# A trunk of two layers on one NeuronCore: the last four weight units of three stages taken tile by tile, with the next stage's norm and transposes between them

## What is computed

```python
def rmsnorm(x, g):
    xf = x * lax.rsqrt(jnp.mean(x * x, axis=-1, keepdims=True) + EPS)
    return xf * g
x = x + conv_ssd_mixer(rmsnorm(x, g0), ...)          # ends in  mixed @ w_out
x = x + swiglu(rmsnorm(x, g1), w_gate, w_up, w_down) # ends in  hidden @ w_down
x = x + diff_attention(rmsnorm(x, g2), ...)          # begins with h @ w_qkv, ends in o @ w_o
h = rmsnorm(x, g3)
logits = h @ w_router                                # 8 experts, the top 2 of each token
x = x + moe_swiglu(h, logits, w_gate_e, w_up_e, w_down_e)
```

## Time and profile before

| | |
|---|---|
| median of 3 runs | 2142.2 us (2140.28 to 2142.95) |
| the profiled execution, its own time | 2140.16 us |
| its span, first to last instruction | 2138.4 us |
| TensorE matmul busy | 2063.0 us, 96% of the span |
| TensorE weight load busy | 1863.9 us |
| VectorE, ScalarE, GpSimd busy | 523.8, 451.5, 487.4 us |
| mean granted TensorE clock | 0.989 of full speed |

### The profile page before, as it was taken

The page is one execution under the profiler, slowest core; times in us unless marked ns, Lnnn a source line. Parts: engine busy times, 40 slices in busy tenths (PEclk is TensorE's granted clock), DMA queues, the critical chain, the costliest instruction groups (busy, mean ns, idle before and its releaser), DMA issues. The chain is left out here.

```text
span 2138.4 us, 32363 instructions
## 1 busy us (share of the span) xinstructions
PE 2063.0 (96%) x13867; PEld 1863.9 (87%) x13867; DVE 523.8 (24%) x987; ACT 451.5 (21%) x896; POOL 487.4 (23%) x246
## 2 busy tenths in 40 slices
PE   7999999999999999988999999999999999999995
PEld 6787778888888878866779999999999999999995
DVE  4534662200000028768340000100101010000102
ACT  4333223332222233358220000000000000000000
POOL 3456564355455434510210000000000000000000
PEclk9999999999999999999999999999999999999998
DMA  7952213233333322310049779888888888898893
GB/s 246 306 163 79 69 59 99 79 100 97 99 94 94 101 83 89 104 35 1 20 168 337 236 251 306 300 304 280 304 282 303 302 300 284 286 310 290 278 343 119
DMA packets 326108, 406.40 MB, mean 190 GB/s; under 512 B 11360, under 2 KB 272554, under 8 KB 325962
## 3 DMA queue, kind: packets, MB, share of 16 engines
q1 hardware_dynamic: 323658, 395.90, 56.1%
q0 software_dynamic: 2304, 8.39, 1.0%
HBM read 373.06 MB, written 31.20 MB: 189 GB/s over the span
## 5 line engine op out<-in xcount | busy, mean ns | idle before, releaser
L875 POOL TENSOR_TENSOR w_lo<-raw,w_hi 128x1024 fp32r<-128x1024 f32 (+1 forms) x159 | 387.9, 2446 | 475.7 <-ACT w_hi L654 475.7
L1456 PE MATMUL ps<-xT,w_gate 128*128 128x132 f32 (+1 forms) x2816 | 356.4, 280 | 4.6 <-issue 3.9
L1456 PE MATMUL ps<-xT,w_up 128*128 128x132 f32 (+1 forms) x2816 | 354.4, 279 | 0.0
L1456 PEld LDWEIGHTS ps<-xT,w_gate 128*128 128x128 f32 x2816 | 340.2, 191 | 5.3 <-issue 4.4
L1463 PE MATMUL ps<-hid,w_down 128*128 128x132 f32 (+1 forms) x2816 | 338.9, 279 | 0.0
L1456 PEld LDWEIGHTS ps<-xT,w_up 128*128 128x128 f32 x2816 | 338.8, 190 | 0.0
L1463 PEld LDWEIGHTS ps<-hid,w_down 128*128 128x128 f32 x2816 | 330.9, 190 | 0.4
L1791 DVE TENSOR_TENSOR hid<-ps,silu_g 128x160 f32<-128x160 f32 x176 | 57.1, 324 | 867.3 <-ACT silu_g L1565 867.3
L1565 ACT ACTIVATE silu_g<-ps 128x160 f32<-128x160 f32 x176 | 53.4, 303 | 934.8 <-PE ps L1456 928.5
L341 PE MATMUL ps<-act_a_hi,w_hi 128*128 128x512 f32 x568 | 226.3, 398 | 0.0
L343 PE MATMUL ps<-act_a_hi,w_lo 128*128 128x512 f32 x568 | 221.2, 390 | 0.0
(11 more groups left out here) (317 smaller groups left out, 2100.6 us busy)
## 6 DMA issues: line engine op xcount, KB each, us to landing
w_gate<-in_moe_w_gate SPq DMA_DIRECT2D x88, 1024.0 KB, 5.5
w_up<-in_moe_w_up SPq DMA_DIRECT2D x88, 1024.0 KB, 8.2
w_down<-in_moe_w_down SPq DMA_DIRECT2D x88, 1024.0 KB, 10.7
raw<-in_even_w_in SPq DMA_DIRECT2D x43, 512.0 KB, 4.3
raw<-in_attn_w_qkv SPq DMA_DIRECT2D x24, 512.0 KB, 3.6
raw<-in_ffn_w_gate SPq DMA_DIRECT2D x22, 512.0 KB, 3.8
raw<-in_ffn_w_up SPq DMA_DIRECT2D x22, 512.0 KB, 3.8
raw<-in_ffn_w_down SPq DMA_DIRECT2D x20, 512.0 KB, 3.7
```

What stands on the lines that cost most here:

```text
L875: pool.tensor_tensor(w_lo[:, u % HL_SLOTS, 0:size(u)], raw[:, u % RAW_SLOTS, 0:size(u)], flat(w_hi[:, u % HL_SLOTS, 0:size(u)]), ALU.subtr ...
L1456: mm = pe.matmul(ps[:, bank, i * CAP:i * CAP + width], w_slots[s][i][:, k, c:c + P], xT[:, k, 0:width], start=(k == 0), stop=(k == KD - 1))
```

## The change

Four things are done.

1. `token_out_last` replaces `token_out` for the last group before each seam. The first units go as before; the last four are taken for tiles 0 and 1 together, then for tile 2 alone, then, after a call `between()`, for tile 3 alone. Only in tile 3's turn are the four units released. `between` transposes the first two tiles of the next stage. VectorE adds and scales by tile (`add_and_norm`), ScalarE squares by tile (`norm_by_tile`), with the splits of the next stage's units between its roots. Groups are renumbered so that the transposes go to banks that the last group doesn't use.
2. `first_two_by_two` takes the place of `first_tokens` at the second seam: each of the first four units for tiles 0 and 1, then tile 2 through four units, then tile 3.
3. The trunk and the experts share one block. The norm of h, its first two transposes and the copies to `hT` move into the trunk's part; `h_tok`, `hT` and the selection matrix get other places. Expert weight slots 2 and 3 swap addresses, and the fourth round's load waits for the scatter and for the picked rows, where before the wait for the scatter came after the fifth round's load.
4. The router takes `hT` as the weight and streams the 8 columns of `w_router`, so its result needs no transposing back. The fillers `keep_clock(18, 0)` (twice) and `keep_clock(7, 0)` go.

```diff
@@ TensorE, trunk
+        def token_out_last(g, u0, depth, source, between):
+            b0, units_in = 4 * (g % 2), (depth + 1) // 2
...
+            for i in range(units_in - 4):
+                begin_unit(u0 + i)
+                for tt in range(NT):
+                    last = add_unit(i, tt)
+                last.then_inc(unit_used, 1)
+            for i in range(units_in - 4, units_in):
+                begin_unit(u0 + i)
+                for tt in (0, 1):
+                    last = add_unit(i, tt)
+                    if i == units_in - 1:
+                        last.then_inc(tile_sum, 1)
+            for i in range(units_in - 4, units_in):
+                last = add_unit(i, 2)
+            last.then_inc(tile_sum, 1)
+            between()
+            for i in range(units_in - 4, units_in):
+                add_unit(i, 3).then_inc(unit_used, 1)
...
-        token_out(G_OUT + 1, U_OUT + 8, 2 * KD, mixed)
-        pe.wait_ge(acc_evac, 4)
-        keep_clock(18, 0)
-        pe.wait_ge(acc_evac, 8)
+        def turn_two(n, freed):
+            pe.wait_ge(acc_evac, freed)
+            turn(n, 0, normed_tile(n))
+            turn(n, 1, normed_tile(n))
+        token_out_last(G_OUT + 1, U_OUT + 8, 2 * KD, mixed, lambda: turn_two(2, 4))
...
-        pe.wait_ge(acc_evac, 20)
-        keep_clock(18, 0)
-        pe.wait_ge(acc_evac, 24)
-        first_tokens(3, U_QKV, normed_tile, act_a_hi, act_a_lo)
+        first_two_by_two(3, U_QKV, lambda tt: pe.wait_ge(acc_evac, 21 + tt))
...
+        def turn_h_two():
+            pe.wait_ge(acc_evac, 44)
+            turn_h(pe, 0)
+            turn_h(pe, 1)
+        token_out_last(G_WO + 1, U_WO + 4, KD, of(act_b_hi, act_b_lo), turn_h_two)
@@ TensorE, second seam
+        def first_two_by_two(n, u0, bank_free):
...
+            turned_parts(n, 1)
+            for i in range(4):
+                begin_unit(u0 + i)
+                for tt in (0, 1):
+                    if i == 0:
+                        bank_free(tt)
+                    add_unit(i, tt)
+                if i < 2:
+                    turn(n, 2 + i, normed_tile(n))
+            for tt in (2, 3):
+                turned_parts(n, tt)
+                bank_free(tt)
+                for i in range(4):
+                    last = add_unit(i, tt)
+                    if tt == 3:
+                        last.then_inc(unit_used, 1)
@@ ScalarE, first and second seam
+        def norm_by_tile(k, n, u0, tile_ready):
...
+            roots(0)
+            roots(1)
+            high(0)
+            high(1)
+            roots(2)
+            high_parts(u0 + 2)
+            roots(3)
+            high_parts(u0 + 3)
+            high(2)
+            high(3)
@@ ScalarE, third seam
+        moe_roots(0)
+        moe_roots(1)
+        keep_hT(0)
+        keep_hT(1)
+        moe_roots(2)
+        moe_roots(3)
+        keep_hT(2)
+        keep_hT(3)
@@ VectorE, first and second seam
+        def add_and_norm(k, g, last_unit):
+            n = (0, 2, 3)[k]
+            dve.wait_ge(gain_in, 16 * (n + 1))
+            for tt in (0, 1):
+                dve.wait_ge(tile_sum, 3 * k - 3 + tt + 1)
+                add_tile(g, tt, 512)
+            norm_tile(k, n, 0)
+            norm_tile(k, n, 1)
+            dve.wait_ge(tile_sum, 3 * k)
+            add_tile(g, 2, 512)
+            turned_low(n, 0, act_a_hi, act_a_lo)
+            turned_low(n, 1, act_a_hi, act_a_lo)
+            norm_tile(k, n, 2)
+            dve.wait_ge(unit_used, last_unit + 1)
+            add_tile(g, 3, 512)
+            norm_tile(k, n, 3)
+            turned_low(n, 2, act_a_hi, act_a_lo)
+            turned_low(n, 3, act_a_hi, act_a_lo)
@@ between trunk and experts
-    block.__exit__(None, None, None)
...
-    block = nc.Block()
-    block.__enter__()
@@ SyncE, experts
                 if u >= WSLOTS:
                     sp.wait_ge(down_done, u - WSLOTS + 1)
+                if u == WSLOTS - 1:
+                    sp.wait_ge(scattered, 16 * 2 * NT)
+                    sp.wait_ge(picked, 3)
                 load_expert_round(sp, e, r, u % WSLOTS)
                 if r == WSLOTS and w + 1 < E:
-                    if w == 0:
-                        sp.wait_ge(scattered, 16 * 2 * NT)
                     sp.wait_ge(x_turned, w * 2 + 2)
@@ TensorE, experts
+        def route(tt):
+            pe.wait_ge(hT_made, 2 * tt + 2)
+            for k in range(KD):
+                mm = pe.matmul(ps[:, 0, 8 * tt:8 * tt + 8], hT[:, k, tt * P:(tt + 1) * P], w_router[:, k, :],
+                               start=(k == 0), stop=(k == KD - 1))
+            return mm
...
-        keep_clock(7, 0)
         pe.wait_ge(moe_in, 16)
-        for tt in range(NT + 1):
...
-        pe.wait_ge(logitsT_copied, NT)
-        for tt in range(NT):
-            mm = pe.transpose(ps[:, 6, 8 * tt:8 * tt + 8], logitsT[0:E, tt * P:(tt + 1) * P], ident[0:E, 0:E])
-        mm.then_inc(routed, 1)
-        keep_clock(2, 0)
+        pe.wait_ge(acc_evac, 45)
+        route(0)
+        route(1)
+        turn_h(pe, 2)
+        route(2)
+        turn_h(pe, 3)
+        route(3).then_inc(routed, 1)
+        keep_clock(2, 1)
```

More of the change, by code:

```diff
@@ L265, in load_expert_round, with turn_h @@
             sp.dma_start(dst[:], src.rearrange("(k p) n -> p k n", p=P)).then_inc(there, 16)
+    def turn_h(pe, tt):
+        pe.wait_ge(h_made, tt + 1)
+        for half in range(2):
+            i = 2 * tt + half
+            if i >= 4:
+                pe.wait_ge(hT_made, i - 3)
+            for j in range(4):
+                c = (4 * half + j) * P
+                mm = pe.transpose(ps[:, 4 + i % 4, j * P:(j + 1) * P], h_tok[:, tt, c:c + P], ident[:])
+            mm.then_inc(h_turned, 1)
     block = nc.Block()
@@ L378, in turn, with normed_tile, first_features @@
                 mm.then_inc(turned, 1)
[L380 to L386, removed]
+        def normed_tile(n):
+            return lambda tt: normed[n][tt % 2]
         def turned_parts(n, tt):
             pe.wait_ge(lo_ev, 8 * n + 2 * tt + 2)
-        def first_features(n, u0):
-            turn(n, 0, normed_tile)
-            turn(n, 1, normed_tile)
+        def first_features(n, u0, bank_free=None):
             for half in range(2):
@@ L698, in norm, with roots, high @@
             turned_high(n, act_a_hi, u0, last_two=lambda: roots((2, 3)))
+        def norm_by_tile(k, n, u0, tile_ready):
+            def roots(tt):
+                tile_ready(tt)
+                root_mean_square(k, tt, ff_gate[:].rearrange("p a b -> p (a b)"))
+            def high(tt):
+                for half in range(2):
+                    i = 8 * n + 2 * tt + half
+                    act.wait_ge(turned, i + 1)
+                    act.activation(act_a_hi[:, 4 * half:4 * half + 4, tt * P:(tt + 1) * P],
+                                   ps[:, TURN_BANK[n] + i % 4, :].rearrange("p (a b) -> p a b", a=4),
+                                   ACT.Copy).then_inc(hi_ev, 1)
+            roots(0)
[8 more added lines that the diff above has]
+            high(3)
         act.wait_ge(pads_ready, 1)
@@ L775, in _ @@
         turned_high(1, act_a_hi, U_OUT)
-        for g in range(2):
-            for i in range(8):
-                high_parts(U_OUT + 8 * g + i + AHEAD)
+        high_parts(U_FF - 1)
         load_root_table()
-        high_parts(U_FF + AHEAD)
-        norm(1, 2, U_FF, lambda tt: act.wait_ge(acc_evac, 5 + tt), ff_gate)
+        norm_by_tile(1, 2, U_FF, lambda tt: act.wait_ge(acc_evac, 5 + tt))
         for half in range(2):
@@ L1121, in _ @@
         add_to_x(G_OUT, U_OUT + 7, 0)
-        add_to_x(G_OUT + 1, U_OUT + 15, 512)
-        norm(1)
+        add_and_norm(1, G_OUT + 1, U_OUT + 15)
         for half in range(2):
```

200 lines of the change are left out of this document (114 added, 86 removed).

## The result

The changed kernel takes **2124.65 us** (median of 4 runs, 2123.63 to 2126.14) against 2142.57 for the kernel before, measured beside it (4 runs, 2140.28 to 2142.95): 17.9 us less, a ratio of 0.9923, interval 0.9911 to 0.9936. That is faster by more than the 0.2% that a measurement can tell. The forecast was 2128.1, the range 2120.5 to 2134.5. The busy shares hardly move: TensorE's matmuls 2051.1 us, 97% of the span, where they were 96%.

The account below looks back on a forecast made before the run. Bound by TensorE up to the router, then the router's chain, then 36.4 us of weight loading. Gains 6.6 + 4.2 + 3.3 = 14.1 took the profiled 2140.16 to 2126.1; 2.0 for the median made 2128.1 us, range 2120.5 to 2134.5.

Parts of the forecast that it names:

- the hole: TensorE's 21.27 us wait for a gate weight load after two rounds of expert weights; forecast to stay as long.
- First seam: Gap before the SwiGLU's first matmul: 9.4 us shrinks to 1.9 of transposes plus 0.9 of waiting, gain 6.6 us.
- Second seam: Gap before the input projection's first matmul: 7.68 us shrinks to 1.9 plus 1.5 of waiting, gain 4.2 us.
- rival 2: First two seams: GpSimd at about 2.9 us a unit makes TensorE wait for each first unit; 2134.1 us, chance 0.15.
- Third seam: From the trunk's end through the router: the order of the experts comes 3.3 us earlier, with the clock falling.
- The clock's fall: In the router: 8-column records drop TensorE to the 1.2 GHz level at about 1074, after tile 2's transposes.
- the ten rank records at half clock add 1: Behind the logits, after two fillers: ten rank records run at half clock and cost 1 us more.
- Rival 1: The clock holds through the router, so the third seam gives 9.6 us; total gain 20.4, 2121.8 us, chance 0.25.
- Rival 3: The fourth round's expert load comes late because the scatter lands late, stopping the weight queue; 2147 us, chance 0.04.
- point of decision: Fourth round's loads must be issued about 15 us before they are wanted; scatter landing after 1132 costs one us each.
- Rival 4: The gain is given back unseen, a tile-order wait misread and the two seams kept; 2141 us, chance 0.04.

Follow-up runs that it names:

- experiment 2: The changed kernel with the router in its old form, 8 columns as the weight and 128 tokens streaming: 2120.13 us, ratio 0.9911 to the kernel before.
- experiment 9: The changed kernel again, word for word, measured and profiled a second time: 2124.44 us, ratio 0.9925 to the kernel before.
- experiment 4: The changed kernel with six 512-column fillers after a tile's router and four after transposes: 2122.0 us, ratio 0.9915 to the kernel before.
- experiment 1: The changed kernel with its first seam as before, 18 fillers included: 2132.37 us, ratio 0.9969 to the kernel before.
- experiment 5: The kernel before without the seven fillers, `keep_clock(7, 0)`, at the start of the experts' block: 2140.12 us, ratio 1.0001.
- experiment 6: The kernel before without the 18 fillers, `keep_clock(18, 0)`, at each of the first two seams: 2141.41 us, ratio 1.0003.
- experiment 3: The changed kernel with three 512-column fillers after each tile's router and each tile's transposes: 2122.34 us, ratio 0.9927 to the kernel before.

## Why the prediction was right, and where not

**What bounds the kernel.** Right: the hole stayed (21.32 us against 21.27), and what came earlier at the first load came out at the end, 15.5 us of the 16.6.

**First seam, 6.6 us.** 6.8 in the trace. The transposes started without a wait and the remaining gap was 0.83 us for a forecast of 0.9, for the reason given. The forecast priced the 16 transposes at their busy time of 1.9 us; from their start to the next matmul they take 1.66 to 1.67, which is 0.2 of the surplus at each seam. One term was off unseen: GpSimd's first unit took 2.79 us, not 2.41. The Trainium skill (GPSIMD Engine Reference, "8. Key points") says that GpSimd shares its SBUF interfaces with VectorE and contends with it where VectorE reads two SBUF inputs; the trace agrees, with 2.79 and 3.37 us for the two units beside VectorE's scaling and 2.36 and 2.35 for the others, but no run separates the cause. Beyond the first unit it cost nothing, since the transposes of tiles 2 and 3 lie between TensorE's units: they start at 409.85, 413.58 and 417.32, 3.7 us apart, not 2.9.

**Second seam, 4.2 us.** 4.4 in the trace, gap 1.40 for a forecast of 1.5. Here too the transposes lie between the units, which start at 778.83, 782.47, 786.11 and 788.83; GpSimd had finished the fourth at 786.77, 2.1 us before it was wanted. So rival 2 did not follow from its own condition: at 2.9 us a unit the fourth would be ready at 787.6, and only the first would be waited for.

**Third seam, 3.3 us.** Up to the first load it was 5.4 (6.2 to the logits, less 0.8 behind them). The clock's fall came as it was put: 4.5 us after the last trunk matmul, after tile 2's transposes (3.4 us behind it and before those transposes in the second profile of the same program). Three terms were off. First, the sum: the terms as written (1069.9 + 3.7 + 0.95 + 0.8 + 3.3 + 1.8 + 0.8 + 3.3 + 0.35) make 1084.9 and not the 1085.5 written, a slip of 0.6 us; the measured stretch is 15.0 us long, as those terms are. Second, the 16 transposes again, 1.67 us for 1.9. Third, "the ten rank records at half clock add 1": the two fillers ahead of them raised the clock, the last six of the records ran in 0.82 us, and only the fillers' own delay (0.8 to 0.9 us for a forecast of 1.05) was paid. The second profile of the same kernel paid some of it, 7.9 us from logits to load instead of 7.3.

**What was left out.** Attention's clock, -1.1 us: the forecast took a part whose instructions don't change for one whose time doesn't change. And +1.3 behind the hole, again the clock. That they nearly cancel is luck; the profile's 16.5 against the forecast's 14.1 is the third seam's 2.1 and the first two's 0.4. The medians differ by 17.9, 1.4 more than the profiled executions, since the profiled execution of before lies 2.4 below the median and that of after 1.0.

**Rival 1, the clock holds.** It did not, in this kernel. The Trainium skill (TensorE: Matmul & The Clock Gate, "What's actually happening") has the gate follow how busy TensorE has been; read as occupied time, that is contradicted by the two stretches of experiment 2 and by the fall in experiment 9, with TensorE busy 3.00 of 3.00 us. No run had its case, the narrow form at full clock without fillers. The nearest are experiment 2, the wide form at full clock (2120.13), and experiment 4, the narrow form held up by fillers (2122.0); its time was 2121.8.

**Rival 3, the fourth load.** Rightly unlikely, but its point of decision was wrong. "About 15 us before they are wanted" came from a load with others queued ahead; alone in the queue, 8.5 us did.

**Rival 4** is excluded by the result, and for the first seam by experiment 1. For the second seam and for the joining of the blocks no run undid the change; the 4.4 us, and what the third seam gave, are read from the two traces.

**Left open.** What sets whether attention's clock falls at 925, and where in the router it falls. The kernel before and experiment 5 are the same program up to the first seam, and the clock fell at that seam in one trace and not in the other; no run controlled this.

## What to carry to other kernels

A seam between two dependent stages can be filled with the last units' own work: take the last few weight units tile by tile, so that most tiles are finished while one is still being multiplied. Then look for what now starts last; here it was the next weights' low half, and one subtraction moved to an engine that was idle gave 2.1 us more at the two seams. Don't turn a small product round to save a transpose without looking at what streams: the 8-column form took nearly the same time per record, let the clock fall and cost 3.8 us up to the first load. And before a gain of one or two us is believed, the same program is worth a second trace: here its stretches moved by as much as 1.35 us.

## What the runs showed of the hardware

- TensorE was granted 0.50 while it was occupied without a gap by 8-column records and their full-size weight loads (3.00 of 3.00 us each), and 1.00 while it was busy 2.80 of 4.00 us with 128-column records. In the second profile of the same program the clock fell within the 8-column records, with TensorE busy 3.00 of 3.00 us from 1059 to 1062.
- The clock came back from 0.50 to 1.00 with nothing but 128x128 float32 transposes since a standstill of 4.81 us (experiment 6, 411.53 to 415).
- At full clock a float32 matmul record of 8 columns takes nearly as long as one of 128: 1.70 us for 16 (experiment 3, 1058.90 to 1060.60) against 1.84 (experiment 2, 1064.80 to 1066.64).
- A 128x1024 subtraction took 1.22 us on VectorE and 2.79 on GpSimd in the same place. GpSimd's took 2.79 and 3.37 us where VectorE's scaling ran beside them and 2.36 and 2.35 where it ran beside less or none of it.
- The clock's falls in attention moved the end of the trunk by 1.1 us between kernels whose instructions there are the same, and by 1.3 us between two profiles of one kernel.
